# Value products of three attention stages turned: values as the stationary operand, probabilities divided before they are transposed

## The reference

```
# latent attention, 8 heads, 256 queries, 256 keys, value width 64
p = softmax(q @ k.T * scale);  o = p @ v
# sparse attention of a later layer, 8 heads in 2 kv groups, block of 128 queries
p_c, p_s, p_w = masked_softmax(...)      # over 15 compressed keys, over the selected blocks, over the window
out = g0 * (p_c @ vc) + g1 * (p_s @ vs) + g2 * (p_w @ vw)
```

## Time and profile before

| | us |
|---|---|
| median of 3 runs (lowest, highest) | 1892.83 (1892.48, 1893.13) |
| the profiled execution itself | 1892.62 |
| its span, first to last instruction | 1890.8 |

### The profile page before, as it was taken

The page is one execution under the profiler, slowest core; times in us unless marked ns, Lnnn a source line. Parts: engine busy times, 40 slices in busy tenths (PEclk is TensorE's granted clock), DMA queues, the critical chain, the costliest instruction groups (busy, mean ns, idle before and its releaser), DMA issues.

```text
span 1890.8 us, 28359 instructions
## 1 busy us (share of the span) xinstructions
PE 1872.9 (99%) x10752; PEld 1616.9 (86%) x10752; DVE 1353.2 (72%) x1729; ACT 840.4 (44%) x1043; POOL 124.3 (7%) x155
## 2 busy tenths in 40 slices
PE   9999999999999999999999999999999999999998
PEld 8998888888888888888888888888888888888887
DVE  5677767776767776775787677677777667777777
ACT  5564434564334533444354533344344335444333
POOL 1002100330000100000300100010000020010000
PEclk9999999999999999999999999999999999999999
DMA  7423555425555565545434465565554444355553
GB/s 305 179 89 147 200 189 189 167 89 207 194 193 198 221 226 181 196 158 184 167 138 146 176 223 180 197 235 224 185 195 172 174 152 154 137 198 202 187 196 115
DMA packets 48548, 343.46 MB, mean 182 GB/s; under 512 B 5472, under 2 KB 5504, under 8 KB 8784
## 3 DMA queue, kind: packets, MB, share of 16 engines
q1 hardware_dynamic: 43200, 310.92, 45.8%
q0 software_dynamic: 5264, 31.35, 4.4%
HBM read 341.20 MB, written 1.05 MB: 181 GB/s over the span
## 4 chain that ended last, share of the span: by engine, by line
PE 65%; DVE 1%; POOL 0%; issue 0%; ACT 0%; DVEq 0%; POOLq 0%
PE bank L1065 16%; PE bank L853 12%; PE bank L855 11%; PE bank L854 11%; PE bank L1064 7%; PE bank L916 2%; PE bank L1170 1%; PE bank L1067 1%; PE bank L1144 1%; PE bank L961 1%; PE bank L956 1%; PE bank L957 1%; DVE rnorm L2662 0%; POOL rstd L704 0%; DVE wlo L2020 0%
## 5 line engine op out<-in xcount | busy, mean ns | idle before, releaser
L2020 DVE TENSOR_TENSOR wlo<-raw,whi 128x2048 fp32r<-128x2048 f32 x292 | 670.3, 2298 | 220.4 <-ACT whi L1558 219.6
L1558 ACT ACTIVATE whi<-raw 128x2048 fp32r<-128x2048 f32 x293 | 559.1, 1909 | 273.7 <-PE bank L855 267.6
L1065 PE MATMUL bank<-ysp,whi 128*128 128x512 f32 x1920 | 666.1, 396 | 0.0
L1064 PE MATMUL bank<-ysp,wlo 128*128 128x256 f32 x1680 | 468.5, 279 | 0.0
L1065 PEld LDWEIGHTS bank<-ysp,whi 128*128 128x128 f32 x1920 | 347.6, 188 | 67.1
L1064 PEld LDWEIGHTS bank<-ysp,wlo 128*128 128x128 f32 x1680 | 316.7, 189 | 10.7
L1641 ACT ACTIVATE sg<-sg 128x256 f32<-128x256 f32 x120 | 50.1, 418 | 468.2 <-DVE sg L2217 468.2
L853 PE MATMUL bank<-whi,ysp 128*128 128x512 f32 (+3 forms) x592 | 217.4, 367 | 2.7 <-DVE nk L2591 2.4
L855 PE MATMUL bank<-whi,ysp 128*128 128x512 f32 (+3 forms) x592 | 212.7, 359 | 0.0
L854 PE MATMUL bank<-wlo,ysp 128*128 128x512 f32 (+3 forms) x592 | 212.4, 359 | 0.0
L853 PE MATMUL bank<-whi,hl 128*128 128x512 f32 x528 | 206.0, 390 | 0.0
(11 more groups left out here) (362 smaller groups left out, 2375.7 us busy)
## 6 DMA issues: line engine op xcount, KB each, us to landing
raw<-stream SPq DMA_DIRECT2D x294, 1024.0 KB, 4.8
sr<-side POOLq DMA_DIRECT2D x10, 1024.0 KB, 5.6
gbc<-gains POOLq DMA_DIRECT2D x11, 512.0 KB, 3.9
cw<-small POOLq DMA_DIRECT2D x2, 2048.0 KB, 10.3
gbias<-gate_rows POOLq DMA_DIRECT2D x6, 512.0 KB, 3.9
dbias<-dilb POOLq DMA_DIRECT2D x1, 2304.0 KB, 13.3
lng<-rows POOLq DMA_DIRECT2D x2, 1024.0 KB, 5.2
tab<-second POOLq DMA_DIRECT2D x1, 1724.0 KB, 15.1
```

What stands on the lines that cost most here:

```text
L1064: pe.matmul(o[:, 0, :], lo[:, k, cols], yh[:, k, :], start=False, stop=False, skip_group_check=True)
L1065: last = pe.matmul(o, hi[:, k, cols], ysp[:, :, k, :], start=k == 0, stop=k == 7)
L1558: act.activation(whi[s], raw[s], ACT.Copy).then_inc(hi_made, 1)
L2020: dve.tensor_tensor(wlo[s], raw[s], whi[s].bitcast(F32), ALU.subtract).then_inc(lo_made, 1)
```

## The change

In the later layers' sparse attention and in the latent attention, the probabilities are divided by their sum (and multiplied by the gate) before they are transposed; the value product has the values as its stationary operand, at one half of the array's columns for one head and the other half for another, and sums over key blocks (in the sparse attention over branches too) in bank 1 or banks 0 and 1. The result stands with its features on the partitions. The rows of two weights are put in another order on the way in. In the projection before it, the drain of step 14 is put ahead of a tile's split.

```diff
-PLAN1.batches("ocat", "B")
-PLAN2.batches("y", "BBBB")
+PLAN2.batches("y", "BB")
...
# PE, attention(): what stands in for the product by heads
                         copied(B, tb + nt)
+                        if summed:
+                            summed(i - 2).then_inc(o_done, 1)
+                            continue
...
# PE, latent attention
-                if i == 4:
+                if i == 5:
                     pe.wait_ge(src_ready, 3)
+                    heads_copied(1)
                     late_batch("cat2", [...])
-                if i == 5:
-                    pe.wait_ge(o_ready, AG_MLA + 2)
-                    late_batch("cat0", [...])
...
+            def heads_summed(i):
+                q, m = divmod(i, 2)
+                g = groups[i]
...
+                for kt in range(2):
+                    for j in range(2):
+                        for e in range(2):
+                            r, c = 64 * e, 256 * j + P * m
+                            last = pe.matmul(pb[q][r:r + 64, c:c + P], g["v"](2 * j + e, kt), g["pt"][:, 2 * j + e, kt, :],
+                                             start=..., stop=..., tile_position=(0, r), skip_group_check=True)
...
# PE, sparse attention
                 for m in range(M):
                     gate_half(m, True)
-                    pe.wait_ge(ce_ready, M * l + m + 1)
+                for m in range(M):
+                    pe.wait_ge(cn_ready, M * l + m + 1)
                     batch(B, tb + m, [P2[0][:, m, 0:120]], 120)
...
-                    pe.matmul(pb[4 + m], PT2[0][0:120, m, 0, :], bd[0:120, :, :]..., start=True, stop=True).then_inc(co_done, 1)
...
+                def compressed_out(m):
...
+                    for r in range(4):
+                        pe.matmul(pb[1][:, r * P:r * P + P], bd[0:120, r]..., cPT[0:120, m, :], start=r == 0, stop=False, ...)
+                def values_summed(i):
+                    m, br, x_ = i // 4, i // 2 % 2, i % 2
+                    if i % 4 == 0:
+                        compressed_out(m)
+                    for kt in range(m + 1):
+                        for b in range(2):
+                            r, c = 64 * b, P * br + 64 * b
+                            last = pe.matmul(pb[1][r:r + 64, 256 * x_:256 * x_ + 256], nv[:, kt, c:c + 64], PT2[i % 2][:, 2 * b:2 * b + 2, kt, :],
+                                             start=False, stop=..., tile_position=(0, r), skip_group_check=True)
...
-                        square(B, tb + 2, lambda m, k: vA[:, m, k * P:k * P + P], 4, 8)
...
# ACT, attention(): p_made after the four exponentials; the division in the sparse attention
+                    if i < n and shared is not None and scaled:
+                        act.wait_ge(share_ready, shared + i + 1)
+                        for h in range(4):
+                            ins = act.activation(g["p"][:, h, 0:g["nk"]], g["p"][:, h, 0:g["nk"]], ACT.Copy, scale=share[:, i % 2, h:h + 1])
                             if h % 2:
                                 ins.then_inc(p_ready, 1)
...
+                def out_high(m):
+                    act.wait_ge(o_done, AG_NSA + 8 * l + 4 * m + 4)
+                    act.activation(cTh[m], pb[1]..., ACT.Copy).then_inc(oT_hi, 1)
...
# DVE, latent attention: the division
-            attention(B, "mla", mla_groups(), AG_MLA, normalize, late_heads_T, ...)
+            def between(i):
+                if i < 4:
+                    dve.wait_ge(p_made, i + 1)
+                    link(dve.reciprocal(share[:, i % 2, :], den[:, i, :]))
+                    p = groups[i]["p"]
+                    dve.tensor_tensor(p, p, bc(share[:, i % 2, :], S), ALU.mult).then_inc(p_ready, 2)
+                if i == 4:
+                    heads_low(0)
+            attention(B, "mla", groups, AG_MLA, None, late_heads_T, between=between)
...
# DVE, sparse attention: in each step after the gates' sum and a tile's split
+                def shares(g, i):
+                    dve.wait_ge(p_made, SHARES_MLA + 8 * l + i + 1)
...
+                    link(dve.reciprocal(share[:, i % 2, :], den[:, i % 4, :]))
+                    part = share[:, i % 2, :].rearrange("p (b h) -> p b h", b=2)
+                    dve.tensor_tensor(part, part, g["gate"], ALU.mult).then_inc(share_ready, 1)
-                def gated(g, i, o):
-                    link(dve.reciprocal(rec, den[:, i % 4, :]))
-                    link(dve.tensor_tensor(rec..., rec..., g["gate"], ALU.mult))
-                    link(dve.tensor_tensor(og2, o, bc(rec, 64), ALU.mult))
-                    link(dve.tensor_tensor(g["out"], g["out"], og2..., ALU.add))
-                    dve.sem_inc(o_ready, 1)
...
# DVE, projection
-                    if i < 16:
+                    if i < 16 and i != 14:
                         ahead(B, "win", i - 1)
...
+                    if i == 14:
+                        ahead(B, "win", 13)
```

More of the change, by code:

```diff
@@ L370, in build @@
         rec = little("rec", 4)
+        share = little("share", 8, (2, 4))
         idle = little("idle", 1)
@@ L612, in mla_groups @@
                         v=lambda h, kt, q=q: mkv[:, kt, 4 * q + h, 64:128], nk=S, p=P0[i % 2], pt=PT0[i % 2],
-                        scale=DK1 ** -0.5, bias=None, out=cat_a[:, m, 256 * q:256 * q + 256].rearrange("p (h d) -> p h d", h=4)))
+                        scale=DK1 ** -0.5, bias=None))
             return out
@@ L1125, in ffn, with attention @@
                     turn(*then, 0, 1)
-            def attention(B, stage, groups, ag0, extra=None, needs={}, turned=None):
+            def attention(B, stage, groups, ag0, extra=None, needs={}, turned=None, summed=None):
                 first_tb, t = [], B.plan.tb[stage]
@@ L1486, in layer @@
                 pe.wait_ge(ro_used, l + 1)
[L1487 to L1490, removed]
                 def gate_step(i):
                     gate_half(2 + i, i < 2)
-                    if i == 0:
-                        pe.wait_ge(yc_ready, 3 * l + 2)
-                attention(B, "nsa", nsa_groups(), AG_NSA + 8 * l, gate_step)
+                def compressed_out(m):
+                    if m == 0:
+                        pe.wait_ge(bd_ready, l + 1)
+                        pe.wait_ge(drain_dve, B.drained(plan.step["gates"] + 3, "D"))
+                    else:
+                        pe.wait_ge(oT_hi, M * l + 1)
+                        pe.wait_ge(oT_lo, M * l + 1)
+                    copied(B, plan.tb["cmp"] + m + 1)
+                    for r in range(4):
+                        pe.matmul(pb[1][:, r * P:r * P + P], bd[0:120, r].rearrange("p g d -> p (g d)"), cPT[0:120, m, :],
+                                  start=r == 0, stop=False, skip_group_check=True)
+                def values_summed(i):
[6 more added lines that the diff above has]
+                            last = pe.matmul(pb[1][r:r + 64, 256 * x_:256 * x_ + 256], nv[:, kt, c:c + 64], PT2[i % 2][:, 2 * b:2 * b + 2, kt, :],
+                                             start=False, stop=i % 4 == 3 and kt == m, tile_position=(0, r), skip_group_check=True)
+                    return last
+                attention(B, "nsa", nsa_groups(), AG_NSA + 8 * l, gate_step, summed=values_summed)
                 tb = plan.tb["y"]
@@ L1665, in ffn, with attention @@
                 pair(B, (NF - 2) * f, NF // 2 - 1)
-            def attention(B, stage, groups, ag0, extra=None, after=None, between=None, copy_leads=()):
+            def attention(B, stage, groups, ag0, extra=None, after=None, between=None, copy_leads=(), shared=None, scaled=True):
                 first_tb, t = [], B.plan.tb[stage]
@@ L2271, in bc, with attention @@
                 return a.unsqueeze(len(a.shape)).broadcast_to(list(a.shape) + [n])
-            def attention(B, stage, groups, ag0, drain, extra=None, before=None, between=None, ends=None):
+            def attention(B, stage, groups, ag0, drain, extra=None, before=None, between=None, ends=None, shares=None):
                 first_tb, t = [], B.plan.tb[stage]
@@ L2301, in attention @@
                         extra(i)
+                    if i < n and shares:
+                        shares(groups[i], i)
                     if 1 <= i <= n:
@@ L2310, in attention @@
                         between(i)
-                    if i >= 2:
+                    if i >= 2 and drain:
                         g, a = groups[i - 2], ag0 + i - 2
@@ L2731, in beside @@
                         gate_sum(2 + i)
-                attention(B, "nsa", nsa_groups(), AG_NSA + 8 * l, gated, beside)
-                dve.sem_inc(yc_ready, 1)
+                attention(B, "nsa", nsa_groups(), AG_NSA + 8 * l, None, beside, shares=shares)
                 tb = plan.tb["y"]
```

137 lines of the change are left out of this document (84 added, 53 removed).

## The result

| | us |
|---|---|
| before: median of 20 runs (lowest, highest) | 1892.82 (1892.39, 1893.13) |
| after: median of 20 runs (lowest, highest) | 1895.62 (1892.75, 1897.49) |
| ratio, 95% interval | 1.0014 (1.0008, 1.0020) |
| span of the profiled execution, before and after | 1890.8, 1895.6 |

The change costs 2.8 us; 8.5 were forecast as a gain, so the forecast is off by 11.3 and its sign is wrong. The median lies inside what was called no change. The runs now lie 4.7 us apart where they lay 0.7 apart, and the mean granted clock goes with the time: 0.999 in the four shortest (up to 1893.37), 0.995 in the four longest (from 1897.36). The profiled execution is the longest of the 20 (1897.49), 1.9 above the median, so its trace shows more trouble than most executions have.

A forecast was written before the change was run, and what follows sets the result against it. PE, busy for 1872.9 of 1890.8 us, was taken to bound the kernel. From 1892.6, less 11.0 for two later layers, plus 2.6 for the latent attention, came 1884.2, stated as 1884.3; range 1880.5 to 1889.5.

The forecast's parts named there:

- what was called no change: Whole kernel: a measured time from 1889.0 to 1896.6 us counts as the same; chance 0.08.
- What bounds the kernel: Whole kernel: PE, busy for 1872.9 of 1890.8 us, sets the time; DVE is busy for 72%, ACT for 44%.
- the value products: Sparse attention: column tiles run side by side, groups take 0.43 and 0.87 us for 0.93 and 1.83; 4.6 saved per layer.
- the mode change: Sparse attention: changing to column tiles costs 0.1 us in each of 8 groups, and 0.2 on leaving the last two.
- (a): Sparse attention's value products: the two column tiles do not run side by side; 10.5 us over both layers, 1895; chance 0.04.
- (b): Value products: only streams overlap, loading the stationary operand stays exposed; 5.3 us in all, 1889.6; chance 0.06.
- The wait on `nk` goes: Projection before the sparse attention: DVE copies 2.2 us sooner, nothing is late next; 1.2 us saved per layer.
- I went through all steps in this way: Sparse attention: PE waits 0.1 at half 2, 0.4 before half 5, 0.7 before half 11, none elsewhere.
- The new waits in the sparse attention: Sparse attention: added DVE and ACT work makes PE wait; 1.2 us lost per layer, bounds none and 3.
- the ring of rival (c): Sparse attention: the chain through ACT and DVE loses 1 us in each of 16 steps, 1900; chance 0.07.
- The latent attention: Latent attention: DVE's division makes its loop 4.9 us a step; 2.6 us lost, bounds 1 and 5.
- Rival (d): Latent attention: PE idles about 2.1, 1.0 and 2.8 us, the clock drops; 4 us more, 1888; chance 0.11.

The follow-up runs named there:

- `nv_first`: Changed kernel with the first half of the projection's last step copied out before the split of the second gates' tile; 1892.62 us.
- `best_nsa`: Changed kernel without the latent attention's part, ScalarE's second probability copy and half of the projection's last drain each put ahead of a split; 1884.32 us.
- `cpt_early`: Changed kernel with ScalarE's copy of the second block's transposed compressed probabilities put ahead of its split for gate half 1; 1892.16 us.
- `best_all`: Whole change plus ScalarE's second probability copy and half of the projection's last drain each ahead of a split, and fillers in the latent attention; 1887.09 us.
- `mla_only`: Kernel before with only the latent attention's part of the change; 1897.2 us, ratio 1.0023.
- `nsa_only`: Changed kernel with the latent attention's part undone, the later layers keeping theirs; 1890.69 us, ratio 0.9991.
- `no_fill`: Kernel before without its seven fillers in step 1 of the latent attention; 1892.51 us.

## Why the prediction was wrong

- **What bounds the kernel, the value products, the mode change:** right. A product took 0.59 and 1.02 us for 0.53 and 0.97; (a) would have been 0.97 and 1.84 and (b) 0.75 and 1.41. The rule of the Trainium skill that stood for (b), in "TensorE: Matmul & The Clock Gate", The mechanism, does not show here either: the tiles share their row groups, and the products took 1.02 and not 1.41. (The same section also lets a load go ahead into a background weight buffer.) The sum lacked a term: the turn from transpositions to products, from record to record, costs 0.20 where it cost 0.11, 0.7 a layer in 8 groups; over half of the 1.2 us that the attention itself fell short.
- **"The wait on `nk` goes ... nothing is late next. Saved: 1.2 us":** this step failed. The first half held, the third line of the table is -2.20 for -2.1. But the working asked when PE needs the tile and not when it needs the bank whose copies stand behind the next split, and it took the splits' durations from where they stood. Moved by 0.6 us against GpSimd (from 0.23 ahead of its first product to 0.37 behind it), they grew from 2.3 and 2.8 to 3.1 and 3.4, the copies that PE needs for gate half 0 came 1.4 late, and PE waited 0.7 (16.78 less the 16.07 of `nv_first`, from compressed to first scores), plus 1.6 where the clock fell behind it.
- **"I went through all steps in this way, each engine's list in order":** it stopped short. The compressed probabilities now have two copies by ScalarE close together ahead of the attention, with a split of 1.9 us between them. The prediction priced the product's matmuls and not what the transpositions wait for: 1.5 us a layer (16.07 less the 14.54 of `best_nsa`), and 3.5 for both layers by the medians of the changed kernel and `cpt_early`. This is the second step that failed.
- **The new waits in the sparse attention:** right, 1.4 a layer for 1.2, at the halves named; the ring of rival (c) isn't there.
- **The latent attention:** the loop was right, 4.9 us from one division to the next (129.46, 134.37, 139.29), and 2.8 us is what it costs at full clock (`best_all`, with its fillers, less `best_nsa`) for 2.6 forecast. Rival (d) had the place and the two long idle stretches (2.1 and 2.8 for 2.09 and 3.20) and was given 0.11; it cost 2.6 by the fillers, not 4. Full clock there was a condition of the forecast, and the longer idle stretches were its own result; that should have raised the chance of (d). The kernel's fillers in that very attention were a weaker hint than they look, as without them the kernel before is no slower.
- **How the losses add:** to the forecast's 1884.2 come 2 x 1.5 that the two best kernels too fell short by (3.99 for 5.5 a layer: 1.2 in the attention, 0.4 ahead of it), 2 x 1.5 for the copy and 2 x 0.7 for the wait before gate half 0: 1891.6, with the clock full. With it falling in the latent attention (2.6) 1894.2, and in both later layers (2 x 1.6) 1897.4. The runs go from 1892.75 to 1897.49; the lowest is under 1894.2, as the latent attention too loses less in some executions (`mla_only` goes from 1895.44 at a mean granted clock of 1.000 to 1898.2 at 0.997). The additions rest on differences of medians and of single traces, so they are good to some tenths. Every rival was priced as the only thing to go wrong.
- **Slips in the working:** the terms of the latent attention's end add up from 145.2 to 149.1, not 149.3 (149.70 in `best_all`), and by the stated bounds the range would end at 1880.2 and 1890.2. Neither changes the outcome.

## What to carry to other kernels

When an instruction is moved ahead of another on one engine, work out again when the second starts, beside what it then runs, and what is copied out behind it; a duration taken from its old place holds only for that place. In a kernel whose PE is busy at 99%, a new wait can cost more through the clock than by itself (here 0.7 us, and 1.6 on top where the clock fell), and a spread of the runs that grows, here from 0.7 to 4.7 us, can be its sign when no slice of the page shows it. A change that loses can hold a gain: undo the parts and put single orders right before giving it up (here 1884.3 and 1887.1 against 1895.6).

## What the runs showed of the hardware

- The clock falls at some times and not at others at the same instructions: 0.77 and 1.00 over 7.3 us in two layers of one execution of `nsa_only`, 1.6 us apart; means of 0.995 to 0.999 over the 20 runs of the changed kernel.
- Products on column tiles of 64 columns run in pairs over 256 columns each, at 0.145 us a record with the changes of mode (13.9 us over 96), also when all records of one tile are issued ahead of the other's (1.02 us for 4 and 4 either way).
- VectorE's split of 2048 numbers goes from 2.28 to 3.06 and 3.37 us beside GpSimd's products of 512 numbers, and these from 1.27 to 3.33.
- Fillers can be worth something or nothing: 19 transposition-sized matmuls that compute nothing took 2.6 us off the changed kernel, where the clock fell in its idle stretches; the seven of the kernel before take nothing off (`no_fill`), where it does not fall without them.
